# The first half of one down-projection chunk, loaded from GpSimd in strips of 8 partitions with single-element DMAs between them

## The reference

```python
def moe_ffn(h, w_router, b_router, w1, b1, w2, b2):      # 32 experts, top 4 of them for each token
    logits = jnp.dot(h, w_router, preferred_element_type=jnp.float32) + b_router.astype(jnp.float32)
    top_logit, top_e = lax.top_k(logits, TOP_K)
    gate = jax.nn.softmax(top_logit, axis=-1)
    ...
    def expert_block(acc, xs):
        tok, g, e = xs
        u = jnp.dot(h_pad[tok], w1[e], preferred_element_type=jnp.float32) + b1[e]
        y = jnp.dot(clamped_swiglu(u).astype(h.dtype), w2[e], preferred_element_type=jnp.float32) + b2[e]
        return acc.at[tok].add(y * g[:, None]), None
```

## Time and profile before

| what | value |
|---|---|
| median of 3 runs | 1048.02 us (1047.65 to 1048.06) |
| profiled execution, span | 1047.2 us |
| TensorE busy | 1028.6 us, 98% |
| VectorE, ScalarE, GpSimd busy | 221.6, 117.5, 0.2 us |
| moved by DMA | 424.62 MB, mean 405 GB/s |

### The profile page before, as it was taken

The page is one execution under the profiler, slowest core; times in us unless marked ns, Lnnn a source line. Parts: engine busy times, 40 slices in busy tenths (PEclk is TensorE's granted clock), DMA queues, the critical chain, the costliest instruction groups (busy, mean ns, idle before and its releaser), DMA issues.

```text
span 1047.2 us, 11219 instructions
## 1 busy us (share of the span) xinstructions
PE 1028.6 (98%) x4918; PEld 417.3 (40%) x4918; DVE 221.6 (21%) x584; ACT 117.5 (11%) x223; POOL 0.2 (0%) x4
## 2 busy tenths in 40 slices
PE   9999999999999999999999999999999999999996
PEld 7888543333333333333333333333333333333332
DVE  2174442111111111111111111111111111111111
ACT  2031121000000000000000000000000000000002
POOL 0000000000000000000000000000000000000000
PEclk9999999999999999999999999999999999999999
DMA  9992899999999999999999999999999999999995
GB/s 319 368 370 81 331 367 412 414 428 425 435 434 427 432 429 434 429 434 429 432 431 429 434 427 432 430 435 429 429 431 429 432 430 432 431 429 426 428 422 223
DMA packets 35958, 424.62 MB, mean 405 GB/s; under 512 B 3160, under 2 KB 15968, under 8 KB 19392
## 3 DMA queue, kind: packets, MB, share of 16 engines
q1 hardware_dynamic: 35600, 423.51, 96.2%
q10 hardware_dynamic: 304, 0.33, 0.1%
HBM read 422.78 MB, written 1.05 MB: 405 GB/s over the span
## 4 chain that ended last, share of the span: by engine, by line
PE 89%; DMA 9%; SPq 1%; another core or an unknown queue 0%; DVE 0%; issue 0%; ACT 0%; DVEq 0%; ACTq 0%
PE PS L1477 38%; PE PS L1500 19%; DMA ring<-in_w 9%; PE PS L1146 8%; PE PS L1446 5%; PE PS L1428 5%; PE PS L1325 3%; PE PS L1283 3%; PE PS L1535 2%; PE PS L1438 2%; PE PS L1420 1%; DMA ring<-in_w_in 1%; SPq L464 0%; PE PS L1608 0%; PE PS L1622 0%
## 5 line engine op out<-in xcount | busy, mean ns | idle before, releaser
L1477 PE MATMUL PS<-ring,work 128*64 128x512 f32 x1976 | 434.0, 596 | 5.7 <-DMA ring<-in_w 5.2
L1477 PEld LDWEIGHTS PS<-ring,work 128*64 128x64 f32 x1976 | 139.5, 137 | 277.2 <-issue 266.8
L1500 PE MATMUL PS<-ring,work 128*64 128x512 f32 x1024 | 227.6, 595 | 1.6 <-DMA ring<-in_w 1.6
L1500 PEld LDWEIGHTS PS<-ring,work 128*64 128x64 f32 x1024 | 72.2, 137 | 154.1 <-issue 149.0
L1035 DVE TENSOR_SCALAR work<-PS 128x512 f32<-128x512 f32 x32 | 22.1, 692 | 385.4 <-PE PS L1477 385.4
L1146 PE MATMUL PS<-ring 128*128 128x256 f32 x384 | 85.4, 380 | 1.4 <-DMA ring<-in_w_in 1.4
L669 ACT ACTIVATE work<-work 128x512 f32<-128x512 f32 x32 | 20.2, 630 | 523.5 <-DVE work L1035 523.5
L1146 PEld LDWEIGHTS PS<-ring 128*128 128x128 f32 x384 | 72.0, 190 | 11.9 <-DMA ring<-in_w_in 1.8
L1000 DVE TENSOR_TENSOR work<-PS,n2w 128x512 f32<-128x512 f32 x30 | 20.8, 692 | 228.5 <-PE PS L1438 228.5
L1446 PE MATMUL PS<-late,work 64*128 64x512 f32 x248 | 61.9, 616 | 0.0
L1428 PE MATMUL PS<-resid,work 128*64 128x512 f32 x248 | 58.5, 592 | 0.0
(11 more groups left out here) (176 smaller groups left out, 385.7 us busy)
## 6 DMA issues: line engine op xcount, KB each, us to landing
ring<-in_w SPq DMA_DIRECT2D x72, 4096.0 KB, 35.1
ring<-in_w SPq DMA_DIRECT2D x35, 2048.0 KB, 13.7
ring<-in_w SPq DMA_DIRECT2D x22, 1024.0 KB, 8.5
ring<-in_w_in SPq DMA_DIRECT2D x11, 1024.0 KB, 12.0
ring<-in_w_out SPq DMA_DIRECT2D x4, 1024.0 KB, 12.1
ring<-in_w SPq DMA_DIRECT2D x6, 512.0 KB, 6.9
ring<-in_w_in SPq DMA_DIRECT2D x2, 512.0 KB, 7.3
ring<-in_consts SPq DMA_DIRECT2D x1, 800.0 KB, 12.2
```

The costliest lines, as they stand in the source:

```text
L1477: last = mm(bank(b0 + v)[64 * half:64 * half + 64, :], rows[:, c, :], turned_half(w[:, v * F:(v + 1) * F], half), start=(second and c == 0 ...
L1500: last = mm(out[64 * half:64 * half + 64, :], aT_n[:, c, 64 * h:64 * h + 64], ring[:, 2 * d + c // 2, cols:cols + BANK], start=(h == 0 and ...
```

## The change

GpSimd gets a program. It waits for the same `chunk_used` count as SP does for chunk (31, 4), then issues sixteen pairs of DMAs: one of eight single elements (a column of 8 partitions of the constants, into one of the unused columns of `stat`), and one of 8 partitions of the half, 8 rows of 8 KB. SP leaves out its DMA of this half in the main round and still issues the second half. TensorE waits for all sixteen strips, 16 x 16 in place of 16. At its end GpSimd waits for the sixteen small DMAs. In further rounds, which run only if an expert has more than 64 tokens, SP loads the half as before.

```diff
+STRIP = 8
+STRIPS = P // STRIP
+IN_STRIPS = (LAST, W1_CHUNKS)
+SPACER_COL = 40
...
+        spacer_in = sem("spacer_in")
...
                     src = w2_half(e - 1, down_chunk(j, k))
-                    sp.dma_start(dst[:, 0:2 * D], src[:, 0:2 * D]).then_inc(half_in[END_HALVES.index((j, k))], 16)
+                    if not (isinstance(r, int) and (j, k) == IN_STRIPS):
+                        sp.dma_start(dst[:, 0:2 * D], src[:, 0:2 * D]).then_inc(half_in[END_HALVES.index((j, k))], 16)
                     sp.dma_start(dst[:, 2 * D:], src[:, 2 * D:]).then_inc(pair_full[d], 16)
...
+        @block.gpsimd
+        def _(pool):
+            j, k = IN_STRIPS
+            d = pair_of(j, k)
+            dst = ring[:, 2 * d, :]
+            src = w2_v[j - 1, :, 0:SLOT_COLS]
+            pool.wait_ge(chunk_used, HEAD_CHUNKS + place_in_stream(j, k) - PAIRS + 1)
+            for n in range(STRIPS):
+                a = n * STRIP
+                at = SPACER_COL + n
+                pool.dma_start(stat[0:STRIP, at:at + 1], consts[0:STRIP, 0:1]).then_inc(spacer_in, 16)
+                pool.dma_start(dst[a:a + STRIP, :], src[a:a + STRIP, :]).then_inc(half_in[END_HALVES.index((j, k))], 16)
+            pool.wait_ge(spacer_in, 16 * STRIPS)
...
-                pe.wait_ge(half_in[END_HALVES.index((j, k))], 16 * (r + 1))
+                loads = STRIPS if (j, k) == IN_STRIPS else 1
+                pe.wait_ge(half_in[END_HALVES.index((j, k))], 16 * (r + loads))
```

## The result

The changed kernel takes 1065.39 us (median of 4 runs, 1063.2 to 1065.7) against 1047.95 for the kernel before in the same job: ratio 1.0162, 95% interval 1.015 to 1.0175, so 17.4 us slower. The forecast was 1052.2 with a range up to 1060: the sign was right, the size was not, and the range missed it. The profiled execution is the fastest of the four, 1063.2 us with a span of 1061.4, which is 14.2 us more than the span before. The time is 1.8 us above the span here, and 1048.95 against 1047.2 in a later run (one DMA of 128 partitions).

A forecast was written before the change was run, and what follows sets the result against it. A backlog of weight loads was taken to pace the end. Tolls of 6.4 us, with 2.46 us less or more per engine half and a 4.5 us lead, gave about +4.2 on 1048.0: 1052.2 us, range 1046.3 to 1060.

The forecast's parts named there:

- What bounds the kernel: Last stretch of the kernel: a backlog of weight loads paces the end; last loads later by x delay it almost x.
- The issue on GpSimd: GpSimd's 32 DMAs from about 970: 1 us each, 32 us in all, done at about 1003, before the need at 1018.52.
- The landing I took at 2 us: GpSimd's DMAs: some 2 us of flight for the last one, within the 48 us before TensorE needs the half.
- rival D: GpSimd's issue is the bound: at 1.8 us per DMA the last strip lands 11 us late; +9, 1057 us; chance 0.10.
- The toll per lone arrival: DMA engines, beside SP's stream: each lone packet from GpSimd costs 0.4 us, 16 per engine, 6.4 us more.
- rival E: All 16 DMA engines pay the 0.4 us for all 32 DMAs: +10 to +17 us, 1058 to 1065; chance 0.10.
- The sign that was to show the toll: DMA windows between 970 and 1003: share staying at 1.0 while the rate falls from about 426 to some 340 to 350 GB/s.
- the other sign named: SP's queue: its own packets slowing for the whole stretch would show the forecast wrong altogether.
- The main case's last step: End of the loads: the later engine half, about +4.2 us, is added to 1048.0, giving 1052.2 us; chance 0.34.
- Placement: DMA engines: spacers put all strips on one half of them, which carries 2.46 us more, the other 2.46 us less.
- Rival A: Toll only 0.01 to 0.04 us, strips on the leading engine half: TensorE's waits mostly go, 1046.4 us; chance 0.22.
- The floor of 1.88 us of removable waits: TensorE's three late waits for weights: if every load came early, the end comes 1.88 us earlier, no more; 1046.1 us.

## Why the prediction was wrong

**What bounds the kernel: right.** The transfers pace the end, and a lower rate from 970 on came out at the end nearly one for one: 13 us of bytes lacking, 14.2 us of span. One premise was not: in the changed kernel the last parts have no wait before them, and the last wait is the one at 1031.90, for the last chunk of w1.

**The issue on GpSimd: mis-sized, without effect.** 0.51 us each instead of 1. The landing I took at 2 us was 20 in the median. The last strip was issued at 1024.21, past the 1018.52 at which TensorE wanted it before; but TensorE was itself 17 us behind by then, reached it at 1035.38 and didn't wait. The trace shows no case in which rival D decided.

**The toll per lone arrival: the failed step.** The sum's main term was 16 x 0.4 us for arrivals, read off the instruction queue's row. Sixteen spacers alone cost 0.1 us, and one DMA with 128 lone data packets costs 0.0. The nearer row was the other one, the ACT queue's with 0.01 us. The fetches' row is a price of fetches: it says what their own packets take, not what any packet on another queue takes. That 0.4 x 32 = 12.8 would have given nearly the right total is chance: rival E, at +10 to +17 us, had nearly the right number (+17.4) and the wrong reason, since half of its 32 arrivals are free and the other half are as well if they come as one DMA of 128 partitions. The sign that was to show the toll came all the same: share 1.0 at 365, 334 and 351 GB/s between 970 and 1000, where 340 to 350 were forecast. It cannot tell a toll from slower packets; the other sign named, SP's own packets slowed for the whole stretch, is what happened: between 980 and 990 SP's queue takes 94.5% for 3.13 MB in the changed kernel, 48.3 us of engine time per MB, where it took 37.6 before (101.2% for 4.31 MB). The main case's last step is also loose: the later of +3.9 and +4.4 is +4.4, not 4.2.

**Placement: priced at 2.46 us a half, and the wrong thing was placed.** I counted bytes per engine only. There is a second count, bytes per way into SBUF: the 64 KB of a strip enter by what serves 8 adjacent partitions. The reading that fits the runs is that in a load of 128 partitions each engine has its own way in, and a row that comes in by another engine's way holds up both. The runs show its effects (partitions 0 to 63 nothing, 64 to 127 +3.2, with both queues' bytes slowed; destination spread +7.1, source spread +16.5); which engine wrote where is not shown. The rule on the ways in stood in the Trainium skill (SBUF — State Buffer, Door 1: the DMA port swizzle); the prediction weighed two rules of its DMA page and not this one, though a DMA of 8 partitions is what it is about.

**Rival A: did not come.** Its small toll was right, but no split gained. To relieve the late half, a row of its partitions must be carried by an engine of the other half, and that row then meets the owner's stream. The runs with rows for both halves of the partitions, cut finer than 128, all lost. That no split can gain by this is argued, not tried.

**The clock: missing from the working, not from the time.** 6.2 of the 15.4 us on TensorE are matmuls at a lower clock after waits. I took waits at their own length. Reading the waits alone, one finds 11.1 - 1.9 = 9.2 us of the loss and misses the rest; but as the transfers set the end, the slower matmuls took the place of waiting. In this trace the next 16 matmuls took 5.35 to 6.48 us after the waits of 2.40 us and more, and 3.65 after those of 1.85 us and less. The length of the last wait does not decide it alone: with SP's adjacent strips they took 5.35 after 1.94 us (5.35 also the time before, after 4.62), and with SP's spread strips 8 took the usual 1.94 after a wait of 2.11. The floor of 1.88 us of removable waits was not tested by anything.

## What to carry to other kernels

Before a large DMA is cut, ask through which partitions each piece enters SBUF, not only how many engines carry it: cut it along the free dimension, in the number of elements per partition, and keep all 128 partitions in each piece, as this kernel does with its halves. A DMA share of 1.0 with a fallen GB/s says that packets take longer; divide each queue's share by its MB to see whose, and look then at destinations. And behind a full stream of loads, reckon the loss from the transfers: TensorE's waits and its slower matmuls after them share the same time.

## What the runs showed of the hardware

- The same 1 MB beside a full stream costs 0 us as one DMA of 128 partitions, 5.9 to 7.1 us as DMAs of 64 or 32 adjacent partitions or of 8 that lie 4 apart, and 15.5 to 17.4 us as DMAs of 8 adjacent ones, the last from GpSimd as from ScalarE. In SP's own stream DMAs of 8 cost 8.7 us adjacent and 6.8 spread.
- From ScalarE, eight DMAs of 8 partitions that lie 4 apart cost 4.0 us more for partitions 64 to 127 than for 0 to 63; the bytes of both queues then take 51 us of engine time per MB in place of 38.
- Sixteen DMAs of eight single elements on GpSimd's queue: 0.52 us of issue each, and +0.1 us of time (0.9995 to 1.0014).
- GpSimd's queue took 31 of 32 DMAs at once and held the last: for 39.4 us in the changed kernel, 30.6 with spread strips, 7.2 with the spacers first; with 16 there was no such wait. That it waited for room is inferred.
- The same 16 matmuls: 3.65 us, and 5.35 to 6.48 after waits for weights of 2.28 to 4.71 us in the changed kernel and the run without spacers, in windows with a granted clock of 0.72 to 0.94.
